# Reordering the RWKV levels, the odd layer's input projection and its delta passes in a two-layer hybrid trunk

## What is computed

```python
c_b, c_c, c_x, dn_qkv, dn_z, dn_beta, dn_alpha = split(h @ w_in)
y_c = c_b * conv3_centred(c_c * c_x, conv_c)
qkv = silu(conv3_centred(dn_qkv, conv_dn))
q, k = l2norm(q) * HEAD_DIM_D ** -0.5, l2norm(k)
# per direction and chunk: lhs = I + tril(k k^T * beta * decay), solved for u
# o = (q * exp(gc)) @ state + (q k^T * decay) @ u;  state += (k * decay)^T @ u
y_d = rmsnorm(o, dn_norm) * silu(dn_z)
```

## Time and profile before

| | us |
|---|---|
| median of 3 runs | 1800.96 |
| the profiled execution's own time | 1797.01 |
| its span in the trace | 1795.3 |
| TensorE busy in the span | 1704.0 |
| VectorE busy | 1306.4 |
| ScalarE busy | 967.0 |
| GpSimd busy | 78.9 |
| mean granted TensorE clock | 0.963 |

### The profile page before, as it was taken

How to read it: one execution, slowest core, us unless ns; L and a number is a source line. 1 busy time by engine, 2 the same in 40 slices (tenths; PEclk the granted TensorE clock), 3 DMA queues, 4 the chain that set the end, 5 groups by cost and what they waited for, 6 DMA issues and landing times.

```text
span 1795.3 us, 22588 instructions
## 1 busy us (share of the span) xinstructions
PE 1704.0 (95%) x8728; PEld 1414.3 (79%) x8728; DVE 1306.4 (73%) x1232; ACT 967.0 (54%) x905; POOL 78.9 (4%) x92
## 2 busy tenths in 40 slices
PE   7998999999999956989999999999999999999997
PEld 3867988699988835668888888888888888888886
DVE  5587555544430677468898888898888988888985
ACT  2455221444331231157767677777677677677773
POOL 1013321000000003000000000000000000000000
PEclk9998888999999988989999999999999999999999
DMA  6410002455542310089999999999999999999992
GB/s 230 136 59 0 1 1 94 140 184 185 190 169 94 141 47 1 7 287 372 369 334 367 376 330 362 352 353 366 336 363 375 322 369 375 326 368 353 346 372 100
DMA packets 199502, 428.78 MB, mean 239 GB/s; under 512 B 10746, under 2 KB 34574, under 8 KB 199438
## 3 DMA queue, kind: packets, MB, share of 16 engines
q1 hardware_dynamic: 199438, 427.90, 66.3%
HBM read 426.82 MB, written 1.05 MB: 238 GB/s over the span
## 4 chain that ended last, share of the span: by engine, by line
PE 91%; DVE 6%; ACT 1%; issue 1%; POOL 0%; DMA 0%; SPq 0%; DVEq 0%; ACTq 0%
PE bank L2416 17%; PE bank L2418 17%; PE bank L2417 17%; PE bank L2252 5%; PE bank L2185 4%; PE bank L2186 3%; PE bank L2184 3%; PE bank L2425 2%; PE bank L1842 2%; PE bank L2015 2%; PE bank L1833 2%; PE bank L2359 2%; PE bank L2154 2%; PE bank L2461 1%; PE bank L2030 1%; PE bank L2027 1%
## 5 line engine op out<-in xcount | busy, mean ns | idle before, releaser
L1778 DVE TENSOR_TENSOR split<-ring,split 128x2048 fp32r<-128x2048 f32 x336 | 763.8, 2289 | 113.3 <-ACT split L1051 109.7
L1051 ACT ACTIVATE split<-ring 128x2048 fp32r<-128x2048 f32 x336 | 640.2, 1924 | 175.5 <-PE bank L2418 173.9
L2416 PE MATMUL bank<-split 128*128 128x512 f32 x896 | 354.4, 395 | 2.7 <-DVE split L1752 1.4
L2418 PE MATMUL bank<-split 128*128 128x512 f32 x896 | 349.6, 390 | 0.0
L2417 PE MATMUL bank<-split 128*128 128x512 f32 x896 | 348.9, 389 | 0.0
L2416 PEld LDWEIGHTS bank<-split 128*128 128x128 f32 x896 | 168.3, 188 | 36.4 <-issue 1.7
L2418 PEld LDWEIGHTS bank<-split 128*128 128x128 f32 x896 | 168.2, 188 | 35.9
L2417 PEld LDWEIGHTS bank<-split 128*128 128x128 f32 x896 | 168.5, 188 | 33.5
L2416 PE MATMUL bank<-split,ehr_ 128*128 128x512 f32 x448 | 180.3, 402 | 0.0
L2418 PE MATMUL bank<-split,ehr_ 128*128 128x512 f32 x448 | 174.9, 391 | 0.0
L2417 PE MATMUL bank<-split,ehr_ 128*128 128x512 f32 x448 | 174.6, 390 | 0.0
(11 more groups left out here) (461 smaller groups left out, 2153.3 us busy)
## 6 DMA issues: line engine op xcount, KB each, us to landing
ring<-in_od_moe_gate SPq DMA_DIRECT2D x112, 1024.0 KB, 7.0
ring<-in_od_moe_up SPq DMA_DIRECT2D x112, 1024.0 KB, 7.3
ring<-in_od_moe_down SPq DMA_DIRECT2D x112, 1024.0 KB, 6.6
ring<-in_od_w_in SPq DMA_DIRECT2D x7, 2048.0 KB, 7.8
ring<-in_ev_w_in SPq DMA_DIRECT2D x6, 2048.0 KB, 9.0
ring<-in_ev_ffn_gate SPq DMA_DIRECT2D x11, 1024.0 KB, 5.4
ring<-in_ev_ffn_up SPq DMA_DIRECT2D x11, 1024.0 KB, 7.9
ring<-in_ev_ffn_down SPq DMA_DIRECT2D x5, 2048.0 KB, 7.9
```

The source lines that it names most:

```text
L1051: act.activation(wst[:, r % NSTAGE, 0, :], ring[:, (r % NHALF) * HALF:(r % NHALF + 1) * HALF], ACT.Copy).then_inc(w_hi, 1)
L1778: dve.tensor_tensor(wst[:, r % NSTAGE, 1, :], ring[:, (r % NHALF) * HALF:(r % NHALF + 1) * HALF], wst[:, r % NSTAGE, 0, :].bitcast(F32), S ...
L2416: pe.matmul(o, hi, wh, start=start, stop=False)
L2418: return pe.matmul(o, lo, wh, start=False, stop=stop)
```

## The change

In RWKV: the identity of the block inverses is set between two heads' scores and in memory of its own; `attended` leaves `block_inverses`; for pass 0 the level matrices are masked by GpSimd without waiting for the block inverses; `expand` is split in a P and a T part that are issued for the next pass as soon as its target is free; the remainders come between X and PT of the last level; `outputs_v` (the part of the outputs without U) comes ahead of U; `mask_scores` 2 comes after the last `inv_adds`; `score(3)` uses the banks in another order. In the odd layer: projection pieces in the order `OD`=(3, 4, 1, 2, 0, 5), by half pieces over two banks, with everything else of the delta rule set between them; the centre tap of the convolutions moves to ScalarE; norms are taken with one-hot columns (8 x 256 values, a root and a reciprocal of these alone, and a product that spreads them); the four transposing gathers of 32 partitions become 16 ScalarE copies and one transpose; passes 4 and 5 have all weighing ahead of the levels, outputs ahead of states, and the product of keys and state between levels 4 and 5 of pass 5.

```diff
+OD = (3, 4, 1, 2, 0, 5)
@@ gpsimd level_masks
-                        elif p % 4 == 0:
+                        elif p == 0:
+                            pool.wait_ge(vt_sb, 2)
+                            pool.wait_ge(q_rdy, 4)
+                            pool.wait_ge(dve_step, DVE_STEPS["bon_cp"])
+                        elif p == 4:
                             pool.wait_ge(dve_step, DVE_STEPS[blocks])
@@ scalar
+                def tile_copies(t):
+                    act.wait_ge(cv_ps, t + 1)
+                    n = OD[t // 2]
...
+                        act.activation(qkvr[:, m:m + 2, :], src, ACT.Copy)
+                        for i in range(2):
+                            last = act.activation(qkvc[:, m + i, :], src[:, i, :], ACT.Copy, scale=cols[:, b:b + 1])
...
+                for i in range(4):
+                    act.wait_ge(ao_rdy, i + 1)
+                    for k in range(4):
+                        r = slice(32 * k, 32 * k + 32)
+                        last = act.activation(strided(Qc2[r], 4 * i, (16, 2), (32, 32), (1, 4)),
+                                              strided(Ao[r], 512 * i + 32 * k, (0, 2), (1, 32), (P, 4)), ACT.Copy)
+                    last.then_inc(qc_rdy, 1)
@@ vector, RWKV
+            for g in range(2):
+                expand_p(0, g, Pc)
+            for g in range(2):
+                expand_t(0, g, Tc)
+                attended(g)
...
+                if p == 0:
+                    for g in range(2):
+                        expand_t(1, g, Tc)
+                    states(p, z)
+                    evacuated(p, c)
+                    for g in range(2):
+                        dve.wait_ge(u_ps, g + 1)
+                        expand_p(1, g, Pc)
@@ vector, odd layer
+                for g in range(2):
+                    expand_p(4, g, Pc2)
+                for g in range(2):
+                    expand_t(4, g, Tc2)
+                late_convs()
+                for p in range(4, 6):
+                    for g in range(2):
+                        weigh(p, g)
+                dve.wait_ge(tk_sb, 4)
@@ tensor, RWKV
+                    if lev == NLEV - 1:
...
+                        for g in range(2):
+                            rests(p, g)
+                    for g in range(2):
...
+                        level_pt(p, lev, g)
                 if p < 2:
+                    outputs_v(p, 0)
+                    outputs_v(p, 1)
+                    updates(p, 0)
+                    updates(p, 1)
                     pe.wait_ge(tok_sb, 2 * p + 2)
+                    states_v(p, 0)
+                    states_v(p, 1)
+                    states_u(p, 0)
+                    states_u(p, 1)
                 else:
+                    outputs_v(p, 0)
+                    updates(p, 0)
+                    updates(p, 1)
+                    outputs_v(p, 1)
+                outputs_u(p, 0)
+                outputs_u(p, 1)
@@ tensor, odd layer
+                def od_pair(t):
+                    n = OD[t // 2]
                     w8 = weights("od_in", n).rearrange("p (k n) -> p k n", k=KT)
+                    if t >= 2:
+                        pe.wait_ge(cv_sb, t - 1)
+                    for f in range(2):
+                        c = P * (2 * (t % 2) + f)
                         for k in range(KT):
+                            last = pe.matmul(B[t % 2][:, SEQ * f:SEQ * f + SEQ], w8[:, k, c:c + P], hT[:, k, :],
+                                             start=(k == 0), stop=(k == KT - 1))
+                    last.then_inc(cv_ps, 1)
...
+                        if p == 5 and lev == LEV0:
+                            keys_state(0)
+                            keys_state(1)
```

More of the change, by code:

```diff
@@ L1418, in ln_apply, with evacuated @@
                 dve.tensor_tensor(y1, y1, xn[:, c, WA:2 * WA], ADD).then_inc(dve_step, 1)
[L1420 to L1444, removed]
+            def evacuated(p, c):
                 for g in range(2):
@@ new lines, in level_x @@
+                n = inv_seq(p, lev, g)
+                if lev == LEV0:
+                    pe.wait_ge(ex_p, 2 * p + g + 1)
+                else:
+                    pe.wait_ge(tp_sb, n - 2)
+                pe.wait_ge(am_rdy, n)
+                pm = odd_even(Pm[g], lev, True)
+                for u in range(4):
+                    if lev == NLEV - 1 and INV[p][g][0] == 0:
+                        o, i = B[g][:, P * u:P * u + 64], pm[:, u, 0, :]
+                    else:
+                        o, i = B[g][:, P * u:P * u + P], Pm[g][:, u, :]
+                    last = pe.matmul(o, Am[g][:, u, :], i, start=True, stop=True)
@@ new lines, in level_x, with level_pt @@
+                last.then_inc(x_ps, 1)
+            def level_pt(p, lev, g):
+                Tm, Pm, Xm, Am = INVB[p]
+                end, z = lev == NLEV - 1, INV[p][g][0]
+                if lev == LEV0:
+                    pe.wait_ge(ex_t, 2 * p + g + 1)
+                pe.wait_ge(x_cp, inv_seq(p, lev, g))
+                xm = odd_even(Xm[g], lev, True)
+                tm = odd_even(Tm[g], lev, False)
+                for u in range(4):
+                    if not (end and z == 1):
+                        last = pe.matmul(packed(B[2 + g], lev, 0)[:, u], Tm[g][:, u, :], xm[:, u],
+                                         start=True, stop=True)
+                    if not (end and z == 0):
+                        last = pe.matmul(packed(B[2 + g], lev, 64)[:, u], Xm[g][:, u, :], tm[:, u],
+                                         start=True, stop=True)
+                last.then_inc(pt_ps, 1)
@@ new lines, in _ @@
+                od_pair(7)
+                pe.wait_ge(kk2_sb, 2)
+                for i in range(2):
+                    turn_tokens(i, 4)
+                for t in range(8, 12):
+                    od_pair(t)
+                pe.wait_ge(ao_rdy, 4)
+                w8 = weights("od_in", 6).rearrange("p (k n) -> p k n", k=KT)
+                for a in range(TT):
+                    for k in range(KT):
+                        last = pe.matmul(B[4 + a][:, :], hT[:, k, P * a:P * a + P], w8[:, k, :],
+                                         start=(k == 0), stop=(k == KT - 1))
+                    last.then_inc(z_ps, 1)
@@ new lines, in updates_o @@
+                def updates_o(p, g):
+                    pe.wait_ge(or_rdy, 2 * (p - 4) + g + 1)
+                    pe.wait_ge(tp_sb, inv_seq(p, NLEV - 1, g))
+                    if p == 5:
+                        pe.wait_ge(os_sb, g + 1)
+                    for u in range(4):
+                        last = pe.matmul(B[6 + g][:, P * u:P * u + P], inverse(p, g)[:, u, :], Ro[g][:, u, :],
+                                         start=True, stop=True)
+                    last.then_inc(ou_ps, 1)
```

716 lines of the change are left out of this document (393 added, 323 removed).

## The result

The changed kernel takes 1734.71 us, the median of 4 runs (1728.78 to 1737.76), against 1801.24 for the kernel before (4 runs); the ratio is 0.9635, 95% interval 0.9605 to 0.9666. 1736 was forecast, 1726 to 1757 the range. The profiled execution took 1728.78 us for its span of 1727.1, where the span before was 1795.3; 1732.0 was expected of it. The runs of the same kernel beside the experiments lie between 1788.92 and 1818.71, so a few us can't be told from none by whole times.

The account below looks back on a forecast made before the run. TensorE bounds nearly everywhere, at a few places waiting on VectorE chains. RWKV 28.7 plus odd layer 39.5 is 68.2 us, 65 after allowances: 1732.0 for the profiled execution, 1736 for the median, range 1726 to 1757.

Parts of the forecast that it names:

- its allowances: Whole sum: taken off 68.2 us are 1 for the clash, 1 for a cold clock, 1.2 for late copies and adds.
- Start: RWKV before pass 0: blocks ready 3.6 us earlier and a shorter first P tile bring the first X 4.8 us earlier.
- The clash with GpSimd: RWKV start: GpSimd's first masks beside the block inverses cost 0 to 2.8 us, taken as 1.
- Passes: Four RWKV passes, each priced by pass 3 at full clock without idle: 105.9 us against 129.8, 23.9 less.
- What covers the stalls that go: RWKV passes: moved remainders, `outputs_v`, the state's V part and mask 2 hide TensorE's waits, within the 23.9 us.
- the clock doesn't stay up: Rival, RWKV passes: short gaps suffice to lower the clock, 17 of 23.9 us lost again, 1753 us; chance 0.13.
- The norms change nothing in it.: Odd layer: new norms leave TensorE's 114.4 us before pass 4's first X unchanged, 8 products of 512 columns becoming 16 of 256.
- VectorE against z: Odd layer after pair 7: VectorE's chain of 37.5 to 40.3 us fits beside TensorE's 43.2 with 3 to 6 spare.
- the rival's 1.2: Rival, VectorE holds up pass 4: scattered ScalarE copies at 1.2 us each, 13 us lost in all, 1749; chance 0.18.
- Passes 4 and 5: Odd layer: 43.7 us of work plus 0.9 for waits, 44.6 against 52.3, 7.7 us less.
- Pairs in two banks in turn did not swing the clock: Rival, odd projection: cycling PSUM banks puts twelve pairs at half clock, costing 83 us, 1819; chance 0.01.
- nothing was given back later: Rival, experts: the gain is given back there, 1801 us; chance 0.01.

Follow-up runs that it names:

- cover_undone: Changed kernel with the remainders put back behind the last PT and `outputs_v` behind the updates; 1733.46 us (0.9654).
- waits_only: Kernel before with one wait split, so the RWKV remainders wait only for their own scores' masks, nothing reordered; 1775.13 us (0.9833).
- norms_ones: Changed kernel with the norms' lengths taken over the matrix of ones again; 1733.87 us (0.9587), and 1726.13 (0.9579) when run again.
- stall_back: `cover_undone` with the wait for all masks put back ahead of the remainders and the third mask ahead of the last adds; 1761.16 us (0.9752).
- odd_alone: Changed kernel with the RWKV part of before, so only the odd layer is new; 1770.31 us (0.9791).
- rows128: Changed kernel with the eight products that spread the norms' reciprocals made over 128 rows instead of 8; 1729.47 us (0.9593).

## Why the prediction was right, and where it was not

The time came within 1.3 us, and part of that is luck: the sum before its allowances, 68.2 us, is what the span lost, but its terms were off by -1.4 (start), +1.8 (RWKV passes), +3.8 (a stretch that nobody edited), -6.9 (the way to the first X of pass 4), +2.5 (passes 4 and 5) and +0.2. So the profiled execution came 3.2 us below its forecast, 1728.78 for 1732.0, and the median lies 5.9 us above it instead of 4.0.

- *Start, 4.8 forecast, 3.4 measured.* The blocks were ready 2.3 us earlier (169.53 for 171.87) instead of 3.6. The clash with GpSimd took 1.0 of the difference, the size taken for it, on another instruction than the expands. TensorE's last idle time before the first X is 0.62 and stands against ScalarE's copies, but the first P tile itself was ready at about 170.5 (169.53 and a third of 2.94), so the copies can have cost 0.2 at most.
- *Passes, 23.9 forecast, 25.7 measured.* Each came 0.3 to 0.7 below its price (28.4, 27.3, 24.7, 23.6), and pass 3, from which all were priced, was itself at 0.98. The sum is right and the cause is wrong: the step that failed is "What covers the stalls that go". Putting the remainders and `outputs_v` back costs nothing (`cover_undone`); the narrowed wait gives 21.5 us alone (`waits_only`), and by the traces another 2.2 (pass 0, 30.60 to 28.40) go with the cold start behind the wait of 4.83 us for GpSimd, which is gone. The rival "the clock doesn't stay up" named the mechanism, short gaps, and lost because the gaps were gone.
- *"The norms change nothing in it."* This is the failed step of the odd layer: 121.2 us, not 114.4. The prediction counted 8 old products of 512 columns, where the 8 are instructions and the products 4, so the new form has twice the columns. It adds 3.6 of work, and 3.4 of clock. Without them the stage measured 114.19 and 113.91, so the rest of that sum is confirmed, and so is that nothing holds the pairs up. For the same reason it is 163.3 us from the odd projection's start to the output projection, where the prediction said 157 to 162.
- *VectorE against z.* TensorE never waited. VectorE's chain took 39.2 us (587.77 to 626.98), within the 37.5 to 40.3, and ended 0.8 us before the first X of pass 4. That margin was not what the X hung on: it needs the expands, which were done at 613.9, 14 us before. The copies into scattered places took 0.66 each, between the 0.4 estimated and the rival's 1.2, and pair 7's copy came 2.4 us after its pair, which nobody waited for. ScalarE's timeline of the changed kernel:

```profile
576.55 10.57 ACT L988 ACTIVATE ehf<-arena 32x256 f32<-32x256 f32 x16
587.14 0.60 ACT L932 ACTIVATE scr<-bank 128x512 f32<-128x512 f32 x1
```

- *Passes 4 and 5, 44.6 us forecast, 42.13 measured.* The two waits of 0.9 in sum didn't come. Three of the six X take 1.79 instead of 2.01, those that don't stand directly behind the PT of the level before; that is 0.7 of the other 1.6 us, and the rest was not looked for. Two of the chain's pieces (start, us, what), one of each kind:

```profile
648.05 1.79 PE bank L2109 x16
...
660.68 2.01 PE bank L2109 x16
```

- *Not foreseen:* the 3.8 us in the unedited stretch, which took 235.7 us at a clock of 0.96 in the profile of before and 231.3 to 233.7 in every other. With what the passes gave more than forecast (1.8 and 2.5) they made up for the norms and the start. Pairs in two banks in turn did not swing the clock (0.98 over the whole stage in `norms_ones`), and nothing was given back later (1057.15 us behind pass 5 against 1057.34).

## What to carry to other kernels

Before reordering, look at what each wait counts: a wait for all of a semaphore where the reader needs the first part was worth 21 us, most of what the rewrite gained in the RWKV passes and a third of all it gained. Price a short gap of TensorE not by its length alone but also by the cold stretch that may follow (here it followed most of them, not all), and compare kernels by stages between the same two instructions when their starts vary. Count the columns that products stream, from the code, not the instructions of a row; and expect that products over few rows can cost the clock of the work behind them.

## What the runs showed of the hardware

In `stall_back` three gaps of 1.6 to 1.7 us each were followed, within 2 us of their ends and with TensorE full in between, by stretches at half clock that cost 21.5 us in sum. Gaps of 1.86 us (`odd_alone`), 1.95 us (`rows128`) and 1.74 us (before) were not. The clock also fell with no gap at all, during 8 products that read 8 rows; over 128 rows the same products took 3.45 us instead of 4.70 and the clock stayed at 1.00. A VectorE instruction on 128x2 elements took 1.12 instead of 0.17 us beside GpSimd's mask of 128x512 (1.25 each).
